# Two expert layers: blocks of 32 tokens for blocks of 64, spread context steps, first rows by a one-hot product, weights fetched in the order of first use

## The chip, the cores and the metric

The kernel runs on one NeuronCore of a Trainium2 chip. The metric is the time of one launch in microseconds (us), as the device counts it; lower is better. TensorE (PE in the profile) multiplies matrices, VectorE (DVE) and ScalarE (ACT) do elementwise work, GpSimd (POOL) issues the gathers and scatters, and SyncE (SP) issues all other transfers. Everything is fp32.

## The reference, cut to what matters

Two transformer blocks run one after the other over 512 tokens of width 1024. The first ends in an expert layer; the second has a mixer over a short context sequence and the tokens, and then an expert layer of its own. Both expert layers have 32 experts in 4 groups. A token picks one group and two experts in it, so there are 1024 assignments, and each is a gated product through three matrices of 2 MiB:

```python
grp = argmax(logits_c)                       # 1 of 4 groups
top_val, top_idx = top_k(logits_f[grp], 2)   # 2 of its 8 experts
gate = softmax(top_val) * w_grp
y[tok] += gate * ((silu(x @ w_gate[e]) * (x @ w_up[e])) @ w_down[e])
# w_gate, w_up: (32, 1024, 512); w_down: (32, 512, 1024)
```

For the inputs of the reference the experts get from 12 to 49 rows in the first layer, and from 1 to 100 in the second, where five get more than 64.

## The kernel before, in words

The program is written engine by engine: each engine has its own list of instructions, and semaphores tie the lists together. A weight matrix of an expert is one 2 MiB transfer on SyncE's queue into one of several buffers. In the first layer (`m = 0`) these are the six buffers of `ring`, so two experts' weights fit; in the second layer (`m = 1`) four areas of `arena` join them, which makes ten. `STREAM[m]` (line 214) is the order of the 96 transfers of a layer and `SPOT` (line 224) says which buffer each takes; `load_e` (line 1293) waits until the buffer's last user is done and issues the transfer. That last user is the gate and up product of the expert's last block for a gate or up matrix, and the down product for a down matrix (`spent`).

**Blocks.** `BLOCKS[m]` is a fixed list of blocks of `CAP` = 64 rows, each belonging to one expert position: 32 blocks in the first layer, 38 in the second, where six positions have two. In the second layer the experts are first ranked by their row counts, so that the large ones take the positions with two blocks (`RANK`, `order`, `homes`); the first three (`FIXED`) keep their places, since their weights are fetched before the counts are known. An expert with more rows than its blocks hold is finished by a loop at the end of the layer, in overflow blocks: every engine goes through `Fori(0, NOV)` with an `If`, and `NOV` is 15. In the profile nothing runs inside that loop.

**One block on TensorE** (`experts` of the tensor list, lines 847 to 946) is: `gate_up` (868, 870), with the weights as the moving operand of 512 columns, gate into partitions 0 to 63 of a PSUM bank and up into 64 to 127; `turn_x` (855), eight transposes of the next block's rows; `down` of the block before (884, 886); `turn_h` (895), four transposes of the hidden rows. ScalarE does the silu (1837), copies the turned hidden rows (1842) and, in the first layer, the result (1831); VectorE multiplies by up (2542), scales the turned rows (2385, 2389) and, in the second layer, takes the result times its share and a gain (2377). GpSimd gathers each block's rows from a copy of the normalized tokens in DRAM (1476) and scatters the results as half rows (1485).

**Beside the first layer** the second block's work on the context sequence runs: `context()` is a generator on each engine, and TensorE, ScalarE and VectorE take two of its 64 steps in every block (`next(beside, None)`).

**Head of a layer.** VectorE and TensorE compute the routing; the first two blocks' token numbers come from a small product (`first_slots`, 1006), GpSimd gathers these rows, and `gate_up(0)` follows. SyncE, after storing the normalized tokens (1363), waits for the second gather before it goes on to the context's transfers (1366 to 1369) or the stream of weights.

**End of a layer.** After the overflow loop GpSimd scatters the last two blocks, SyncE loads the results back by token (`load_y`, 1306), and VectorE adds them to the residual: lines 2604 and 2605 after the first layer, 2816 and 2817 after the second.

## Time and profile before

| | us |
|---|---|
| median of 3 runs | 1801.9 (1799.53 to 1804.74) |
| the profiled execution | 1797.79 |
| its span, first to last instruction | 1796.0 |
| TensorE busy | 1673.9 (93% of the span) |
| VectorE busy | 657.9 (37%) |
| ScalarE busy | 444.3 (25%) |
| granted clock of TensorE, mean | 0.968 of full speed |
| moved by DMA | 519.45 MB, 289 GB/s over the span |

All times in the profile count from the first instruction. The first expert layer lies at about 340 to 876, the mixer of the second block from there to about 1250, the second expert layer to 1772. Matmuls are pipelined, so the time from the start of one to the start of the next says more than the duration shown. An fp32 product is two records, and a line in the profile is that of the kernel before.

### The profile page before, as it was taken

Reading aid. Unit: us, or ns where it says so; the run is one execution under the profiler, and the core shown is the slowest. Engines: PE = TensorE matmul, PEld = TensorE weight load, DVE = VectorE, ACT = ScalarE, POOL = GpSimd, SP = SyncE. Lnnn points to the kernel's source line nnn. Section 1 sums busy time; section 2 is a strip of 40 time slices with the busy share of each in tenths; the row PEclk is TensorE's granted clock in tenths of the full one; section 3 lists DMA queues with packets and bytes.
Section 4 is the critical chain, followed back from the end, with each engine's and each line's share of the span. In section 5 each row is a group of like instructions: output and inputs, shape, how many; then the busy total and the mean of one; then the engine's idle time right before and its main releaser. Section 6 shows DMA issues by size and latency. Waiting matters only on the chain.

```text
span 1796.0 us, 21821 instructions
## 1 busy us (share of the span) xinstructions
PE 1673.9 (93%) x8694; PEld 857.8 (48%) x8694; DVE 657.9 (37%) x1266; ACT 444.3 (25%) x803; POOL 170.5 (9%) x172
## 2 busy tenths in 40 slices
PE   7999999799999999999699997999799999999993
PEld 3455454445445555455345557965433333333331
DVE  3279341432222212122469937542522222221213
ACT  2233771133221112111348412232000000000001
POOL 0000000011111111110000013100111111111100
PEclk9999999799999999999899998999799999999987
DMA  9265531499999999999470191055899999999995
GB/s 366 101 241 182 189 141 47 152 399 402 393 408 405 406 405 399 403 413 410 175 270 1 13 137 48 1 227 216 318 394 396 404 410 399 409 419 411 423 421 214
DMA packets 95324, 519.45 MB, mean 289 GB/s; under 512 B 22509, under 2 KB 28237, under 8 KB 70648
## 3 DMA queue, kind: packets, MB, share of 16 engines
q1 hardware_dynamic: 84024, 500.66, 72.0%
q0 software_dynamic: 11200, 17.39, 2.9%
q8 instruction: 71, 1.16, 0.3%
q14 instruction: 29, 0.24, 0.0%
HBM read 508.19 MB, written 29.15 MB: 299 GB/s over the span
## 4 chain that ended last, share of the span: by engine, by line
PE 69%; DMA 14%; issue 8%; DVE 5%; ACT 2%; SPq 2%; DVEq 0%; POOLq 0%
PE bank L868 22%; PE bank L884 11%; PE bank L461 8%; PE bank L469 7%; DMA ring<-in_w_up 6%; PE bank L825 3%; PE bank L855 3%; DMA ring<-in_w_down 2%; DMA arena<-in_w_down 2%; PE bank L895 2%; PE bank L527 2%; PE bank L692 2%; PE bank L454 1%; DVE arena L2643 1%; DMA ring<-diag 1%
## 5 line engine op out<-in xcount | busy, mean ns | idle before, releaser
L870 PE MATMUL bank<-ring,arena 128*64 128x512 f32 x912 | 413.2, 607 | 0.0
L868 PE MATMUL bank<-ring,arena 128*64 128x512 f32 x896 | 402.9, 603 | 7.9 <-DMA ring<-in_w_up 4.6
L2542 DVE TENSOR_TENSOR arena<-arena,bank 64x512 f32<-64x512 f32 x70 | 48.3, 690 | 557.5 <-ACT arena L1837 557.5
L461 PE MATMUL bank<-arena,ring 128*128 128x512 f32 x560 | 244.6, 593 | 0.0
L868 PEld LDWEIGHTS bank<-ring,arena 128*64 128x64 f32 x896 | 119.7, 139 | 243.3 <-issue 236.7
L884 PE MATMUL bank<-ring,arena 128*64 128x512 f32 x424 | 193.2, 598 | 2.0 <-DMA ring<-in_w_down 2.0
L886 PE MATMUL bank<-ring,arena 128*64 128x512 f32 x424 | 193.2, 598 | 0.0
L1476 POOL DMA_INDIRECT arena<-xnd,smalli x70 | 67.8, 969 | 1051.1 <-PE bank L855 535.3
L1837 ACT ACTIVATE arena<-bank 64x512 f32<-64x512 f32 x70 | 41.3, 590 | 509.9 <-PE bank L870 509.9
L461 PEld LDWEIGHTS bank<-arena,ring 128*128 128x128 f32 x560 | 105.2, 190 | 127.0 <-issue 127.0
L870 PEld LDWEIGHTS bank<-ring,arena 128*64 128x64 f32 x912 | 122.5, 139 | 0.0
L469 PE MATMUL bank<-arena 128*128 128x128 f32 x880 | 112.4, 280 | 0.0
L469 PEld LDWEIGHTS bank<-arena 128*128 128x128 f32 x880 | 103.0, 192 | 18.4 <-issue 16.9
L868 PE MATMUL bank<-arena 128*64 128x512 f32 x224 | 102.2, 610 | 6.1 <-DMA ring<-in_w_up 6.1
L884 PEld LDWEIGHTS bank<-ring,arena 128*64 128x64 f32 x424 | 53.8, 136 | 96.8 <-issue 91.1
L1485 POOL DMA_INDIRECT yd<-arena,smalli x70 | 70.1, 1001 | 301.4 <-DVE arena L2377 159.3
L870 PE MATMUL bank<-arena 128*64 128x512 f32 x208 | 92.0, 595 | 0.0
L855 PEld LDWEIGHTS bank<-mats,arena 64*128 64x128 f32 x560 | 67.0, 199 | 47.2 <-issue 43.2
L855 PE MATMUL bank<-mats,arena 64*128 64x64 f32 x560 | 76.6, 278 | 11.5 <-DMA arena<-xnd,smalli 11.5
L2643 DVE SCALAR_TENSOR_TENSOR arena<-arena,par 128x512 f32<-128x512 f32 x96 | 72.2, 752 | 3.4
L1842 ACT ACTIVATE arena<-bank 128x256 f32<-128x256 f32 x70 | 26.9, 385 | 179.0 <-PE bank L895 178.6
L895 PEld LDWEIGHTS bank<-mats,arena 64*128 64x128 f32 x280 | 38.7, 209 | 55.3 <-issue 55.2
(452 smaller groups left out, 2104.8 us busy)
## 6 DMA issues: line engine op xcount, KB each, us to landing
ring<-in_w_up SPq DMA_DIRECT2D x53, 2048.0 KB, 20.6
ring<-in_w_gate SPq DMA_DIRECT2D x52, 2048.0 KB, 17.6
ring<-in_w_down SPq DMA_DIRECT2D x50, 2048.0 KB, 20.0
arena<-in_w_down SPq DMA_DIRECT2D x14, 2048.0 KB, 36.4
ring<-in_w_mod SPq DMA_DIRECT2D x12, 2048.0 KB, 15.5
arena<-in_w_gate SPq DMA_DIRECT2D x12, 2048.0 KB, 34.6
arena<-in_w_up SPq DMA_DIRECT2D x11, 2048.0 KB, 27.4
ring<-in_w_in SPq DMA_DIRECT2D x10, 2048.0 KB, 17.4
```

The source lines that it names most:

```text
L461: mm = pe.matmul(b[:, 0:n], w[:, k, col:col + P], ap[:, k, :], start=(k == 0), stop=(k == KD - 1))
L469: mm = pe.matmul(hd(b, h), lhs(h) if callable(lhs) else hd(lhs, h), rhs(h) if callable(rhs) else hd(rhs, h), start=True, stop=True)
L825: mm = pe.matmul(banks[t][:, :], yT(k)[:, P * t:P * t + P], w[:, k, :], start=(k == 4), stop=(last and k == ks[-1]), skip_group_check=True)
L855: mm = pe.transpose(XT[:, CAP * c:CAP * c + CAP], xg[u][:, c::KD], M["ident"][0:CAP, 0:CAP])
L868: pe.matmul(GU[0:CAP, :], x, wg_[:, c, :], start=(c == 0), stop=(c == KD - 1), skip_group_check=True)
L870: mm = pe.matmul(GU[CAP:2 * CAP, :], x, wu_[:, c, :], start=(c == 0), stop=(c == KD - 1), skip_group_check=True)
L884: pe.matmul(Y[0:CAP, :], x, wd_[:, c, 0:512], start=(c == 0), stop=(c == 3), skip_group_check=True)
L886: mm = pe.matmul(Y[CAP:2 * CAP, :], x, wd_[:, c, 512:1024], start=(c == 0), stop=(c == 3), skip_group_check=True)
L895: mm = pe.transpose(HT[:, CAP * c:CAP * c + CAP], hb[u][:, c::4], M["ident"][0:CAP, 0:CAP])
L1476: pool.indirect_dma_start(out=xg[u], out_offset=None, in_=xnd[m], in_offset=bass.IndirectOffsetOnAxis(ap=slots_any[:, n:n + 1], axis=0), b ...
L1485: pool.indirect_dma_start(out=halves, out_offset=bass.IndirectOffsetOnAxis(ap=homes_any[:, n:n + 1], axis=0), in_=ys[u], in_offset=None, b ...
L2643: ins = STT(o8, pad[:, j // 3:j // 3 + 8, j % 3:j % 3 + 64], pcol("cw2", 9 * n + j), o8, ALU.mult, ALU.add)
```

## The change

- Blocks hold 32 rows. `gate_up` and `down` use four column groups of 32 and moving operands of 256 columns, where there were two of 64 and 512. `SIZES` gives each position 1 to 4 blocks: 52 in the first layer, 56 in the second. Both layers now rank the experts.
- Rows are gathered, turned, scaled and scattered for four blocks at a time (`QUAD`, 128 rows), whole rows of 4 KB; `take_y` is four copies of 32 rows by 256 columns. The share of an assignment is applied when the results are added.
- The first 64 rows of the experts 0 and 1 come from a product of the normalized tokens with a one-hot matrix (`first_x`), not from a gather.
- The 64 context steps are placed at chosen points of the blocks (`BESIDE`), so that the work per expert position comes out even.
- `STREAM` is sorted by TensorE's first use, in both layers. A down matrix is fetched in two halves per partition.
- `NOV` is 31; overflow blocks have 128 rows. The waits on SyncE for the first gathers are gone; the load into the tokens' buffer waits for the second `first_x` product.

```diff
-CAP = 64
-NOV = 2 * T // CAP - 1
+CAP = 32
+QUAD = P // CAP
+SIZES = [[2, 2, 2, 1, 1] + [2, 2, 1] * 8 + [2, 1, 1],
+         [2, 2, 2, 1, 1, 1] + [3, 1, 4, 1, 3, 1, 3, 1, 3, 1] + [2, 2, 1] * 4 + [2, 2, 1, 1]]
+NOV = 31
+CONTEXT_STEPS = 64
+PLACES = [[(0, "after"), (0, "down"), (0, "turn"), (0, "half")],
+          [(1, "half"), (0, "down"), (1, "down"), (0, "turn"), (0, "after"), (1, "after")]]
...
+        def first_use(m, j, p):
+            return 2 * FIRSTB[m][p] + (3 if j == 2 else 0), j
+        STREAM = [sorted([(j, p) for j in range(3) for p in range(NE)], key=lambda u: first_use(m, *u)) for m in range(2)]
-        SPOT = [0, 1, 2, 3, 4, 6, 7, 5, 8, 9]
+        SPOT = [0, 1, 2, 3, 4, 6, 7, 5, 9, 8]
...
+                def first_x(e):
+                    b = CV.deal(pe, f"first{m}{e}")
+                    if e == 0:
+                        pe.wait_ge(S("placed"), 3 * m + 1)
+                        pe.wait_ge(S(f"xn{m}"), TT)
                     for c in range(KD):
+                        for t in range(TT):
+                            mm = pe.matmul(b[:, 2 * CAP * c:2 * CAP * c + 2 * CAP], xn_tok[:, t, c::KD], in_soon[:, TT * e + t, :],
+                                           start=(t == 0), stop=(t == TT - 1), skip_group_check=True)
+                    mm.then_inc(CV.full, 1)
+                def turn_x(q, half):
+                    pe.wait_ge(S("xs_ready"), 2 * (g0 + q) + half)
+                    if half == 0:
+                        pe.wait_ge(S("gathered"), 16 * (GBASE[m] + q))
+                    for c in range(4):
+                        mm = pe.transpose(hd(XT, c), xg[:, 4 * half + c::KD], M["ident"])
...
                     for c in range(KD):
-                        x = xTs[u][:, CAP * c:CAP * c + CAP]
-                        pe.matmul(GU[0:CAP, :], x, wg_[:, c, :], start=(c == 0), stop=(c == KD - 1),
+                        if c == KD // 2 and beside_now(n, "half"):
+                            next(beside, None)
+                        x = xTs[q % 2][:, P * c + CAP * b:P * c + CAP * b + CAP]
+                        for i, (w, col) in enumerate(((wg_, 0), (wg_, 256), (wu_, 0), (wu_, 256))):
+                            mm = pe.matmul(GU[CAP * i:CAP * i + CAP, 0:256], x, w[:, c, col:col + 256],
+                                           start=(c == 0), stop=(c == KD - 1), skip_group_check=True)
...
+                        for i in range(4):
+                            mm = pe.matmul(Y[CAP * i:CAP * i + CAP, 0:256], x, wd_[:, c, 256 * i:256 * i + 256],
+                                           start=(c == 0), stop=(c == 3), skip_group_check=True)
...
+                first_x(0)
+                homes()
+                pe.wait_ge(V.free, len(V.names))
                 for n in range(last + 1):
                     gate_up(n)
                     if n == 0:
+                        first_x(1)
+                    if n == 1:
+                        spots()
+                    if beside_now(n, "after"):
                         next(beside, None)
+                    half = turns_at(m, n)
+                    if half is not None:
+                        turn_x(n // QUAD + 1, half)
                     if n:
                         down(n - 1)
+                    if beside_now(n, "down"):
+                        next(beside, None)
                     turn_h(n)
+                    if n == 0:
+                        slots()
+                    if beside_now(n, "turn"):
                         next(beside, None)
                 down(last)
...
-                sp.wait_ge(S("gathered1"), 16 * (BASE[m] // 2 + 1))
                 if m == 0:
                     sp.dma_start(hTc, a["ctxT"].rearrange("(c p) t -> p c t", p=P)).then_inc(S("ctx_in"), 16)
                     sp.dma_start(wkc, cols(a["w_in_2"], 2)).then_inc(S("ctx_w"), 16)
                     sp.wait_ge(S("xn_out"), 16 * TT)
+                    sp.wait_ge(CV.full, CV.at("first01"))
                     sp.dma_start(wvc, cols(a["w_in_2"], 3)).then_inc(S("ctx_w"), 16)
                 if m:
-                    sp.wait_ge(S("xn_out"), 16 * TT * 2)
+                    sp.wait_ge(S("x2_out"), 16 * (1 + TT))
                     load_e(1, 8)
...
+                    if p >= FIXED and j == 0:
+                        if p == FIXED:
+                            sp.wait_ge(S("ordered"), m + 1)
+                        expert[p] = sp.value_load(ordt[0:1, r:r + 1], min_val=0, max_val=NE - 1)
                     if m and i == 3 * FIXED:
-                        sp.wait_ge(S("x2_out"), 16 * (1 + TT))
+                        sp.wait_ge(S("xn_out"), 16 * TT * 2)
+                        sp.wait_ge(CV.full, CV.at("first11"))
                     load_e(m, i, expert.get(p))
...
+                    for i in range(4):
+                        ins = A(ys[q % 2][CAP * b:CAP * b + CAP, 256 * i:256 * i + 256], Y[CAP * i:CAP * i + CAP, 0:256],
+                                ACT.Copy)
...
-                chain(TTo(o, o, yg[t][0], ALU.add))
-                TTo(o, o, yg[t][1], ALU.add).then_inc(S("x4_ready"), 1)
+                chain(STT(o, yg[t][0], w12[:, t:t + 1], o, ALU.mult, ALU.add))
+                STT(o, yg[t][1], w12[:, TT + t:TT + t + 1], o, ALU.mult, ALU.add).then_inc(S("x4_ready"), 1)
```

## Rows read from the trace of the kernel before

**Rows 1.** Busy time by stretch: microseconds (count) per engine, granted clock, DMA share, GB/s
```profile
353.00:866.00 513.00, 513.00 (x2796) 260.35 (x2792) 119.18 (x217) 116.86 (x203) 59.00 (x60) 1.00 0.98 395
1500.00:1740.00 240.00, 226.72 (x1082) 89.29 (x1080) 50.85 (x72) 17.54 (x36) 34.33 (x35) 0.97 1.01 416
```

**Rows 2.** Waits of SyncE's queue: waits for whom, total, times, longest
```profile
SPq L1301 <- PE bank L870: 593.7, 59, 24.6
```

**Rows 3.** Groups by line, 1500 to 1760: count, busy, mean, idle before
```profile
L868 PE MATMUL bank<-ring,arena 128*64 128x512 f32 x204 | 92.9, 609 | 5.3 <-DMA ring<-in_w_up 4.6 <-DMA arena<-in_w_up 0.7
```

**Rows 4.** Timeline of TensorE, one block of the first layer: start, duration, line
```profile
837.33 0.64 PE L868 MATMUL bank<-ring,arena 128*64 128x512 f32 x1
...
844.35 2.05 PE L469 MATMUL bank<-arena 128*128 128x128 f32 x16
...
846.33 1.09 PE L855 MATMUL bank<-mats,arena 64*128 64x64 f32 x8
...
847.35 0.64 PE L884 MATMUL bank<-ring,arena 128*64 128x512 f32 x1
...
850.94 0.69 PE L895 MATMUL bank<-mats,arena 64*128 64x64 f32 x4
...
851.56 2.05 PE L469 MATMUL bank<-arena 128*128 128x128 f32 x16
...
853.54 0.64 PE L868 MATMUL bank<-ring,arena 128*64 128x512 f32 x1
```

**Rows 5.** Timeline of TensorE, modulation by four column groups
```profile
178.46 1.93 PE L639 MATMUL bank<-ring,smallf 128*2 128x128 f32 x64
```

**Rows 6.** DMA queues, 330 to 870: packets, MB, share
```profile
q0 software_dynamic: 5040, 8.64, 4.7%
```

**Rows 7.** Timeline at the first layer's head
```profile
342.47 0.69 DVE L2446 TENSOR_TENSOR arena<-par,arena 128x512 f32<-128x512 f32 x1
...
352.31 1.11 PE L868 MATMUL bank<-ring,arena 128*64 128x512 f32 x1 [0.88 <-DVE arena L2385]
...
361.83 0.34 SPq L1301 DMA_DIRECT2D ring<-in_w_up  x1
```

**Rows 8.** Timeline at the second layer's head
```profile
1260.55 1.75 PE L993 MATMUL bank<-arena,mats 128*128 128x128 f32 x8
...
1263.74 0.69 DVE L2446 TENSOR_TENSOR arena<-par,arena 128x512 f32<-128x512 f32 x1
...
1275.72 0.36 SPq L1301 DMA_DIRECT2D arena<-in_w_gate  x1
...
1276.06 1.11 PE L868 MATMUL bank<-ring,arena 128*64 128x512 f32 x1 [1.69 <-DVE arena L2389]
```

**Rows 9.** Groups of the page: busy, mean ns, idle before
```profile
L1842 ACT ACTIVATE arena<-bank 128x256 f32<-128x256 f32 x70 | 26.9, 385 | 179.0 <-PE bank L895 178.6
```

**Rows 10.** Timeline after the first layer
```profile
861.30 0.69 DVE L2542 TENSOR_TENSOR arena<-arena,bank 64x512 f32<-64x512 f32 x1 [13.14 <-ACT arena L1837]
...
870.22 0.69 DVE L2175 TENSOR_TENSOR arena<-arena,smallf 128x512 f32<-128x512 f32 x1 [8.23 <-issue]
...
873.80 0.97 POOL L1485 DMA_INDIRECT yd<-arena,smalli  x1 [5.21 <-ACT arena L1831]
...
879.71 1.28 ACT L1872 ACT_TABLE_LOAD   x1 [6.68 <-issue]
...
883.08 1.28 DVE L2604 SCALAR_TENSOR_TENSOR arena<-ring,smallf,arena 128x1024 f32<-128x1024 f32 x1 [8.31 <-DMA ring<-yd]
...
885.72 1.06 ACT L1876 ACTIVATE arena<-arena 128x1024 f32<-128x1024 f32 x1 [4.73 <-DVE arena L2605]
```

**Rows 11.** Timeline of VectorE at the end
```profile
1766.94 0.75 DVE L2377 SCALAR_TENSOR_TENSOR arena<-bank,smallf,arena 128x512 f32<-128x512 f32 x1 [4.04 <-PE bank L886]
...
1777.13 1.23 DVE L2816 TENSOR_TENSOR arena<-arena 128x1024 f32<-128x1024 f32 x1 [9.44 <-DMA arena<-yd]
...
1787.67 4.99 DVE L2821 SCALAR_TENSOR_TENSOR arena<-arena,smallf 128x1024 f32<-128x1024 f32 x5
```

More of the change, by code:

```diff
@@ L434, in settle, with stores, beside_now, turns_at @@
                 eng.sem_inc(S(f"passed_{eng.engine.name}"), 1)
+        def stores(m, q):
+            return sum(len(range(q % 2, NQ[i], 2)) for i in range(m)) + q // 2
+        def beside_now(n, at):
+            return (n, at) in BESIDE
+        def turns_at(m, n):
+            b = n % QUAD
+            half = b - 2 if n < QUAD else b - 1
+            return half if half in (0, 1) and n // QUAD + 1 < NQ[m] else None
         block = ctx.enter_context(nc.Block())
@@ L1025, in moe @@
                               start=True, stop=True).then_inc(V.full, 1)
-                experts(m)
+                experts(m, homes)
             moe(0)
@@ L1444, in _ @@
             load_e(1, 3)
+            for r in range(QUAD):
+                part, at = slice(CAP * r, CAP * r + CAP), 5 * D + 256 * r
+                sp.dma_start(m5[part], modd[0:1, at:at + 256].partition_broadcast(CAP)).then_inc(S("rows"), 16)
+                sp.dma_start(b5[part], a["bmod"][:, at:at + 256].partition_broadcast(CAP)).then_inc(S("rows"), 16)
             sp.wait_ge(S("outB_ready"), TT)
@@ L1449, in _ @@
             sp.wait_ge(S("y_taken"), BASE[1] + NB[1])
-            for q in range(2):
-                sp.wait_ge(S(f"stored{q}"), 16 * ((BASE[1] + NB[1]) // 2))
+            for u in range(2):
+                sp.wait_ge(S(f"stored{u}"), 16 * stores(2, u))
             sp.wait_ge(S("yd_done"), 2)
@@ L1488, in scatter @@
                         .then_inc(S(f"stored{u}"), 16)
-                for n in range(NB[m] + 2):
-                    if n == 2:
-                        pool.wait_ge(CV.free, CV.at(f"slots{m}"))
-                    if n < NB[m]:
-                        gather(n)
-                    if n == 4:
-                        pool.wait_ge(CV.free, CV.at(f"spots{m}"))
-                    if n >= 4:
-                        scatter(n - 4)
+                pool.wait_ge(CV.free, CV.at(f"slots{m}"))
+                gather(1)
@@ L1500, in experts @@
+                gather(2)
+                pool.wait_ge(CV.free, CV.at(f"spots{m}"))
+                for q in range(3, NQ[m]):
+                    scatter(q - 3)
+                    gather(q)
+                scatter(NQ[m] - 3)
                 baton = S(f"beyond{m}")
@@ new lines, in take_y, with first_x @@
+                    for i in range(4):
+                        ins = TTo(ys[q % 2][CAP * b:CAP * b + CAP, 256 * i:256 * i + 256], Y[CAP * i:CAP * i + CAP, 0:256],
+                                  m5[CAP * i:CAP * i + CAP, :], ALU.mult)
+                    ins.then_inc(S("y_taken"), 1)
+                def first_x(e):
+                    b = take(f"first{m}{e}", CV)
+                    o, o3 = chunks(xTs[0], P)[:, :, 2 * CAP * e:2 * CAP * e + 2 * CAP], [P, KD, 2 * CAP]
+                    ins = TTo(o, chunks(b[:, :], 2 * CAP), bc(gain, 2, o3), ALU.mult)
+                    ins.then_inc(CV.free, 1)
+                    if shift is not None:
+                        own(f"first{m}{e}", CV)
+                        ins = TTo(o, o, bc(shift, 2, o3), ALU.add)
+                        ins.then_inc(S("xs_ready"), 1)
+                    else:
+                        own(f"first{m}{e}", CV)
+                        dve.sem_inc(S("xs_ready"), 1)
@@ new lines, in experts @@
+                dve.wait_ge(S("ranked"), m + 1)
+                dve.sem_inc(V.free, 1)
+                dve.wait_ge(S("gains"), 1 + 2 * m)
+                first_x(0)
+                b = take(f"homes{m}")
+                CP(bc_row, b[:, 0:2 * NE])
+                chain(CP(ordt, b[0:1, 2 * NE:3 * NE]))
+                dve.sem_inc(S("ordered"), 1)
+                dve.sem_inc(V.free, 1)
+                home, cap, many = bc_row[:, 0:NE], bc_row[:, NE:2 * NE], key[:, 0:NE]
+                chain(TTo(many, cnt, cap, ALU.subtract))
@@ L2478, in experts @@
+                o3 = [P, NE, OVER]
+                chain(TTo(over, bc(many, 2, o3), bc(pcol("slot0", 0, OVER), 1, o3), ALU.is_gt))
                 chain(dve.tensor_reduce(nov, over, AX, ALU.add))
```

523 lines of the change are left out of this document (233 added, 290 removed).

## The prediction

> **What bounds the kernel now.** I read the table by stretch first. In the first expert layer TensorE is busy in all of 353 to 866, 513.00 of 513.00 us, at full granted clock; the DMA engines are booked nearly full too, but move 395 GB/s [rows 1]. To see which of the two sets the pace I took the waits of SyncE's queue: it waits 59 times, 593.7 us in all, for TensorE to free a weight buffer [rows 2]. So weights are fetched no faster than TensorE uses them, and the 395 is a demand, not a limit. In 1500 to 1740 of the second layer it is the other way round: TensorE is busy 226.72 of 240 us, the transfers run at 416 GB/s [rows 1], and the gate and up products wait for weights (4.6 us for ring, 0.7 for arena) [rows 3]. I take 416 for what the transfers can do.
>
> TensorE's timeline of one first-layer block shows where its time goes: gate and up 844.35 − 837.33 = 7.02, a context step 1.98, turning rows 1.02, down 3.59, turning hidden rows 0.62, a second step 1.98, from 837.33 to 853.54, or 16.21 us [rows 4]. 32 such blocks are 519 us. The reference's counts matter: in the second layer five experts have more than 64 rows, and all have a block list that holds them before and after, so no overflow block runs in either kernel.
>
> **The change part by part.**
>
> *Blocks of 32 rows.* An fp32 product is two records; I count records. gate_up is now 16 pairs of records of 512 columns, a pair side by side in two column groups, in 7.02 us, and down 8 pairs in 3.59; the difference is 3.43/8 = 0.429 a pair, which leaves 0.15 for the ends [rows 4]. So 512 columns take 0.429 however many column groups run, and 128 a quarter of it, 0.107. What four groups do the modulation shows: 64 records of 128 columns, 16 quads, in 1.93 us, 0.121 a quad [rows 5], 0.013 over 0.107. After the change gate_up is 16 quads of 256 columns and down 8; a quad is 0.215 + 0.013 = 0.228, gate_up 16 × 0.228 + 0.15 = 3.8, down 8 × 0.228 + 0.15 = 2.0 us. Turning hidden rows is half as many transposes, 0.35 for 0.62; rows are turned once for four blocks, eight records of 0.128 (below), 0.26 a block for 1.02. A block costs 6.4 us where it cost 12.25 [rows 4].
>
> First layer: 52 × 6.4 = 333, the 64 steps as before 64 × 1.98 = 127, first_x(1) with 32 products or 64 records at 0.128 (a context step's 2.05/16 [rows 4]) 8.2, slots and spots 4: 472 us of TensorE, for 519. Bounds for a quad: 0.214 (no excess) and 0.27 (the excess grows with the columns, and TensorE's instruction list doubles, whose fetching no row shows). Placing the steps evenly costs nothing by itself: a position of one block gets up to four steps and one of two blocks mostly one, 14 to 15 us each, so that weights can flow steadily.
>
> *The weights.* With 472 us of work TensorE no longer lies above the transfers. 96 matrices of 2.097 MB, 6 of them there at the start, leave 90 × 2.097 = 188.7 MB; the gathers and scatters move 8.6 MB beside them [rows 6], less the two first gathers and the same bytes in whole rows: 8.2. Together 196.9 MB at 416 GB/s, 473 us. The two sums are equal, so the one that starts later decides, and it is the stream.
>
> *The head of the first layer.* The routing ends at 342.47 + 0.69 = 343.2 and gate_up starts at 352.31, after gather, turning and scaling [rows 7]. Ranking is new here and puts three small VectorE operations ahead of the one-hot matrix, 0.9 us: 344. first_x(0) is 64 records; TensorE has just waited, and after such a wait eight took 1.75 us, 0.219 each [rows 8], where 0.128 is the price in full flow. I take 20 at the first and 44 at the second, 10 us (8 and 14 are the ends): 354, scaling 0.7, gate_up(0) at 355, 3 later than now. An expert's first buffers come free with its last block: 3.8, first_x(1) 8.2, turn_h 0.35, down 2.0, a step 2.0, gate_up 3.8 make 375, where the first refill goes out at 361.83 [rows 7]. With 2 us until its packets flow the stream runs from 377, and +473 its last matrix lands at 850. By the new order two down matrices stand behind the last up matrix, 10 us, so that one lands at 840; then come gate_up 3.8, four steps 7.9, two downs 4.0, turn_h 0.35 and 0.9 of handing over: TensorE ends at 857. Four copies on ScalarE instead of one are 4 × 0.385 = 1.5 [rows 9], so ScalarE ends at 858.5 and the scatter is issued at 859.5; it stood at 873.80 [rows 10]: −14.3. Within the stretch copies, multiplications and scalings lie beside TensorE's 6.4 us a block; without that cover the copies alone would cost 1.5 us a block, 78 us.
>
> *The overflow loop* runs with no block in it 31 times instead of 15. It shows as VectorE's 8.23 us and ScalarE's 6.68 us of idle without a releaser [rows 10]: 0.55 and 0.45 a turn, so 17.0 and 13.8 us. VectorE's last multiplication lies about 848 (TensorE has 9 us of other work behind it), so it is out at 865, does what now takes from 870.22 to 874.77 (883.08 less its wait of 8.31) and is ready at 869.4; the loaded results come 9.3 us after the scatter (883.08 − 873.80) [rows 10], at 868.8. So 2604 runs at 869.4 for 883.08. ScalarE comes out at 858.5 + 13.8 + 1.3 for the table load = 873.6, where its line 1876 starts at 885.72 [rows 10]: **−12.1 us**, 2.2 of the 14.3 being the loop's. Bounds: −9 if a turn is dearer in the new code, −14 if it is hidden.
>
> *The second layer.* first_x(0) replaces the first gather: from the one-hot matrix at 1263.74 + 0.69 to gate_up at 1276.06 are 11.6 us [rows 8], about what 64 records and the scaling take by the prices above; no change. The load into the tokens' buffer waits for first_x(1), so the stream's next matrix goes at 1276 + 3.8 + 8.2 = 1288 where it went at 1275.72 [rows 8]; one load passes it, early. Left are 87 matrices and 8.1 MB of rows, 190.5 MB, at 416 GB/s 458 us: 1747. TensorE's work, 56 × 6.4 = 358, fits beside it, and its granted clock would have to fall to 0.78 on the mean before it didn't. Then 2.0 for down, 1.5 for copies and 1 of handing over: the last copy ends at 1751.6, where the last take_y ends at 1766.94 + 0.75 [rows 11], −16.1. Here VectorE takes the results, so its loop begins after them: out at 1768.6, when the results have been back by token since 1751.6 + 9.4 = 1761 (the 9.44 of its wait now). It starts line 2816 at 1768.6 for 1777.13, and its eight additions, all ready, take 8 × 1.28 = 10.3 where 10.54 pass now to line 2821 [rows 11]: **−8.8 us**. The loop gives half of the 16.1 back. What follows is as it was.
>
> *Single edits at little or nothing.* Down in two halves per partition: shorter rows, from nothing to 1% of the stream (5 us a layer), as no row shows its price; I take none. Ranking in the first layer: in the 0.9 above, and homes on TensorE behind first_x. The share is applied where results are added, by an operation of the shape of 2604. The waits that SyncE loses stood ahead of the context's transfers; behind its new waits for first_x queue the weights, counted above. Gathers of four blocks at once are POOL's, a quad ahead of their use, beside TensorE's 25 us a quad.
>
> The sum is −12.1 − 8.8 = −20.9 us. The profiled execution took 1797.79 with a span of 1796.0, so 1775 and 1777; the median of the runs stands 4 above the profiled one, so **1781 us**. For the transfers I allow 395 to 428 GB/s (3% over 416) in the first layer (+25 to −13 us) and, where 416 is the layer's own row, 404 to 428 in the second (+14 to −13). TensorE's and the transfers' equal sums in the first layer add some waiting on either side; a faster stream would be half eaten by the loops. With a quad of 0.214 to 0.25 that makes 1766 to 1797 for this case.
>
> **The rivals.**
> *A, slower: the quad.* If four column groups share less than the modulation shows, a quad of 256 costs 0.28, a third over 0.214, and a block 24 × 0.28 + 0.3 + 0.61 = 7.63 us. TensorE then has 397 + 139 = 536 us in the first layer and ends at 355 + 536 = 891; ScalarE comes through its copies, loop and table at 891 + 16.6 = 907.6, +21.9, less 8.8 for the second layer, which still hangs on weights: +13, **1815 us**. It decides from a quad of 0.27, where the two layers cancel (355 + 523 + 16.6, +8.9). Against it stand 0.121 for 0.107 [rows 5]; for it, that those records have two rows of output and 128 columns, and that twice as many instructions must be fetched. 14%.
> The Trainium skill (TensorE: Matmul & The Clock Gate, Part 3: Packing small matmuls) has three column tiles at 2.38 times and four row tiles at 3.07 times one; by it a quad is, as an estimate, 0.214 × 4/3.07 = 0.28 us, rival A's time. The trace's quad speaks for 3.5 times.
> *B, no change: the ring.* If six buffers can't carry 416 GB/s, because TensorE holds about three and a freed one needs issue and flight, the first layer stays at 395: 498 us from 377 are 875, TensorE ends 7 later at 882, ScalarE is through at 898.6, +12.9, less 8.8: +4, **1806 us**. For it: no stretch of the first layer shows more than 395 [rows 1]; against: SyncE waited for TensorE there [rows 2]. 13%.
> *C, faster: cheap turns.* If a loop's turn costs half in the new code, 2 us come back in the first layer and 7 in the second, where the results by token then come last: 1772. 7%.
> That the change doesn't do what it says would be overflow blocks; the counts exclude them.
>
> **How the numbers follow.** Forecast 66%, A 14, B 13, C 7. 0.3% is 5.4 us, what a measurement can tell; faster means under 1796.5, slower over 1807.3. The forecast (but 1 in 100) and C are faster: 0.73; B mostly the same: 0.13; A slower: 0.14. The range must leave out 2 in 10: 1760 (a stream of 428 in both layers) to 1808, with B in and A out.
>
> **What would show it.** Right: quads start every 0.23 us and a block takes 6.4; the first layer moves 410 to 420 GB/s with TensorE waiting for weights now and then; gate_up(0) at 355 and the first refill at 375; last scatter at 860; VectorE idle 17 us without a releaser after each layer, ScalarE 14; the second layer's additions begin at 1756.5 (1768.6 less the 12.1 won before). Wrong: quads of 0.27 and a SyncE that still waits for TensorE all the time (A), 395 GB/s with both waiting (B), a turn of the loop far from 0.55, a first refill past 380, or a second layer whose stream falls under 404.

## The result, and the profile after

The changed kernel takes 1838.61 us (median of 4, 1831.76 to 1840.74) for 1801.76: a ratio of 1.0197, with a 95% interval of 1.0166 to 1.0228. It is slower by 37 us where a gain of 21 was forecast. The profiled execution has a span of 1838.1 us for 1796.0, and its milestones show where the 42 us arise. The forecast's own times stand in the middle; from the second layer on they count on its new clock, 12.1 us earlier. The rank product is TensorE's first product in a layer's ranking of the assignments; the head of a layer is counted from it.

| us from the first instruction | before | forecast | after |
|---|---|---|---|
| first layer: rank product | 339.7 | – | 344.0 |
| first layer: gate_up(0) | 352.3 | 355 | 365.8 |
| first refill of a weight buffer | 361.8 | 375 | 394.9 |
| last scatter issued | 873.8 | 859.5 | 896.9 |
| ScalarE goes on behind the layer | 885.7 | 873.6 | 910.2 |
| second layer: rank product | 1260.0 | – | 1288.3 |
| second layer: gate_up(0) | 1276.1 | 1263.9 | 1310.4 |
| load into the tokens' buffer | 1275.7 | 1275.9 | 1331.4 |
| last result taken | 1767.7 | 1739.5 | 1804.2 |
| additions begin | 1777.1 | 1756.5 | 1819.7 |

First the table by stretch, with the columns of [rows 1]:

```profile
340.00:400.00 60.00, 54.48 (x376) 47.15 (x380) 21.07 (x84) 6.29 (x17) 1.19 (x1) 0.63 0.44 153
356.00:386.00 30.00, 29.44 (x169) 26.49 (x168) 8.20 (x25) 0.38 (x1) 0.00 (x0) 0.61 0.01 2
400.00:880.00 480.00, 432.41 (x5714) 282.17 (x5710) 106.02 (x207) 168.17 (x394) 23.65 (x23) 0.97 0.99 407
1302.00:1331.00 29.00, 28.22 (x162) 25.00 (x161) 8.84 (x26) 0.38 (x1) 0.00 (x0) 0.62 0.00 1
1360.00:1780.00 420.00, 337.83 (x4948) 196.53 (x4940) 138.42 (x298) 32.70 (x100) 24.19 (x24) 0.89 1.01 423
```

And the kernel before in the stretches that answer to the first and the fourth of these:

```profile
340.00:400.00 60.00, 52.60 (x300) 27.76 (x301) 23.29 (x73) 16.02 (x27) 7.83 (x8) 0.86 0.85 325
1264.00:1302.00 38.00, 29.67 (x219) 15.76 (x218) 19.52 (x55) 1.56 (x3) 5.26 (x5) 0.81 0.85 299
```

Inside the layers the transfers are what was hoped for in the second, 423 GB/s, and near it in the first, 407. But for some 30 us at each head they stand still, 2 and 1 GB/s, while TensorE is busy nearly all of the time, at a granted clock of 0.61 and 0.62. The kernel before moved 325 GB/s in 340 to 400, where 153 are left, and 299 over its second head. TensorE's timeline of the first head, which answers to [rows 7], and SyncE's first refill say what it is busy with:

```profile
344.04 0.77 PE L1028 MATMUL bank<-arena,mats 128*128 128x128 f32 x2 [5.25 <-DVE arena L2491]
...
348.58 15.52 PE L882 MATMUL bank<-arena 128*128 128x64 f32 x64 [0.23 <-issue]
...
365.83 4.89 PE L911 MATMUL bank<-ring,arena 128*32 128x256 f32 x64 [0.56 <-DVEq L2531]
370.65 15.49 PE L882 MATMUL bank<-arena 128*128 128x64 f32 x64
...
386.49 3.64 PE L943 MATMUL bank<-arena 128*128 128x45 f32 x16
390.06 4.72 PE L911 MATMUL bank<-ring,arena 128*32 128x256 f32 x64
...
398.87 3.66 PE L911 MATMUL bank<-ring,arena 128*32 128x256 f32 x64
...
403.11 1.93 PE L927 MATMUL bank<-ring,arena 128*32 128x256 f32 x32
```

```profile
386.23 0.37 SPq L1407 DMA_DIRECT2D arena<-in_w_in  x1
394.85 0.34 SPq L1327 DMA_DIRECT2D ring<-in_w_gate  x1
...
405.10 0.38 SPq L1327 DMA_DIRECT2D ring<-in_w_down  x1
413.02 0.35 SPq L1327 DMA_DIRECT2D ring<-in_w_gate  x1
```

L882 is first_x, 64 records, 15.5 us each time; L911 is gate_up, L943 the product for the slots, L927 down. No weight buffer is free until the second block of expert 0 is through gate_up, at 394.7. In steady flow the quads cost what they were forecast at or a little less: gate_up's 16 take 3.66 us at 398.87, 0.229 each with the ends in it, where 3.8 us were forecast, and down's 8 take 1.93 for 2.0. The second head, in the place of [rows 8]:

```profile
1292.97 15.47 PE L882 MATMUL bank<-arena 128*128 128x64 f32 x64 [0.39 <-DVE arena L2512]
...
1310.39 5.35 PE L911 MATMUL bank<-ring,arena 128*32 128x256 f32 x64 [0.78 <-DVEq L2531]
1315.67 15.48 PE L882 MATMUL bank<-arena 128*128 128x64 f32 x64
```

```profile
1289.18 0.89 SPq L1327 DMA_DIRECT2D arena<-in_w_down  x1
1331.39 0.35 SPq L1327 DMA_DIRECT2D arena<-in_w_gate  x1
1340.11 0.34 SPq L1327 DMA_DIRECT2D ring<-in_w_up  x1
```

Behind the first layer, where [rows 10] stand for the kernel before (VectorE, POOL, ScalarE, then TensorE), and at the end, in the place of [rows 11]:

```profile
902.36 0.69 DVE L2216 TENSOR_TENSOR arena<-arena,smallf 128x512 f32<-128x512 f32 x1 [16.98 <-issue]
```

```profile
896.91 0.96 POOL L1520 DMA_INDIRECT yd<-arena,smalli  x1 [43.97 <-ACT arena L1865]
```

```profile
908.87 1.28 ACT L1913 ACT_TABLE_LOAD   x1 [12.73 <-issue]
```

```profile
915.50 8.37 PE L1067 MATMUL bank<-arena 128*128 128x128 f32 x48 [20.96 <-issue]
```

```profile
1802.48 1.73 DVE L2420 TENSOR_TENSOR arena<-bank,arena 32x256 f32<-32x256 f32 x4 [2.90 <-PE bank L927]
1819.67 1.28 DVE L2867 SCALAR_TENSOR_TENSOR arena<-arena,smallf 128x1024 f32<-128x1024 f32 x1 [15.47 <-issue]
```

The 31 turns of the overflow loop show as 16.98 us on VectorE and, between the last copy's end at 896.1 and 908.87, 12.7 on ScalarE. TensorE has a loop as well, of 20.96 us, and it comes out last: work goes on at 915.50, 5 us behind ScalarE. Before the change it went on 2.4 us behind ScalarE, and waited for that:

```profile
888.12 7.95 PE L1040 MATMUL bank<-arena 128*128 128x128 f32 x48 [15.73 <-ACT arena L1879]
```

### The profile page after: what moved, and what is told of

Same layout as the page of the kernel before. It is cut to its first block, busy times and chain, and to the rows that moved or that the text cites. A ratio compares the mean times of both kernels' runs of the same rounds, so it can differ in the third digit from the quotient of the medians.

```text
span 1838.1 us, 36358 instructions
## 1 busy us (share of the span) xinstructions
PE 1597.6 (87%) x15456; PEld 999.9 (54%) x15456; DVE 706.0 (38%) x1471; ACT 504.5 (27%) x1055; POOL 85.8 (5%) x84
## 4 chain that ended last, share of the span: by engine, by line
PE 55%; DMA 31%; DVE 6%; issue 3%; ACT 2%; SPq 2%; DVEq 0%; ACTq 0%; POOLq 0%
DMA ring<-in_w_up 18%; PE bank L911 12%; PE bank L485 8%; PE bank L493 7%; DMA arena<-in_w_up 6%; PE bank L927 4%; PE bank L882 3%; PE bank L849 3%; PE bank L1283 3%; DMA ring<-in_w_down 2%; DMA arena<-in_w_down 2%; PE bank L716 2%; PE bank L551 1%; PE bank L478 1%; DMA arena<-xnd,smalli 1%
## 5 line engine op out<-in xcount | busy, mean ns | idle before, releaser
L911 PE MATMUL bank<-ring,arena 128*32 128x256 f32 x5664 | 420.1, 416 | 92.7 <-DMA ring<-in_w_up 70.8
L911 PEld LDWEIGHTS bank<-ring,arena 128*32 128x32 f32 x5664 | 218.9, 119 | 225.8 <-issue 136.1
L911 PE MATMUL bank<-arena 128*32 128x256 f32 x1248 | 134.8, 435 | 28.7 <-DMA arena<-in_w_up 14.5
L927 PE MATMUL bank<-ring,arena 128*32 128x256 f32 x2592 | 156.0, 381 | 3.7 <-DMA ring<-in_w_down 3.7
L927 PEld LDWEIGHTS bank<-ring,arena 128*32 128x32 f32 x2592 | 80.8, 110 | 56.5 <-DMA ring<-in_w_down 5.1
L493 PEld LDWEIGHTS bank<-arena 128*128 128x128 f32 x880 | 103.0, 192 | 15.3 <-issue 14.2
L2420 DVE TENSOR_TENSOR arena<-bank,arena 32x256 f32<-32x256 f32 x224 | 94.2, 420 | 39.2 <-PE bank L927 36.0
L1865 ACT ACTIVATE arena<-bank 32x256 f32<-32x256 f32 x208 | 78.0, 375 | 100.1 <-PE bank L927 98.1
L911 PEld LDWEIGHTS bank<-arena 128*32 128x32 f32 x1248 | 67.0, 125 | 58.6 <-issue 41.1
L882 PE MATMUL bank<-arena 128*128 128x64 f32 x256 | 62.0, 438 | 0.6 <-DVE arena L2512 0.4
L882 PEld LDWEIGHTS bank<-arena 128*128 128x128 f32 x256 | 61.3, 335 | 1.6 <-issue 1.6
L935 PEld LDWEIGHTS bank<-mats,arena 64*128 64x128 f32 x216 | 33.6, 203 | 42.8 <-issue 38.2
L849 PE MATMUL bank<-ring,arena 128*128 128x512 f32 x128 | 55.7, 593 | 0.0
L1283 PE MATMUL bank<-ring,arena 128*128 128x512 f32 x128 | 55.6, 592 | 0.0
```

What stands on the lines that cost most here:

```text
L493: mm = pe.matmul(hd(b, h), lhs(h) if callable(lhs) else hd(lhs, h), rhs(h) if callable(rhs) else hd(rhs, h), start=True, stop=True)
L849: mm = pe.matmul(banks[t][:, :], yT(k)[:, P * t:P * t + P], w[:, k, :], start=(k == 4), stop=(last and k == ks[-1]), skip_group_check=True)
L882: mm = pe.matmul(b[:, 2 * CAP * c:2 * CAP * c + 2 * CAP], xn_tok[:, t, c::KD], in_soon[:, TT * e + t, :], start=(t == 0), stop=(t == TT - ...
L911: mm = pe.matmul(GU[CAP * i:CAP * i + CAP, 0:256], x, w[:, c, col:col + 256], start=(c == 0), stop=(c == KD - 1), skip_group_check=True)
L927: mm = pe.matmul(Y[CAP * i:CAP * i + CAP, 0:256], x, wd_[:, c, 256 * i:256 * i + 256], start=(c == 0), stop=(c == 3), skip_group_check=True)
L1283: mm = pe.matmul(banks[t][:, :], y, w[:, k, :], start=(k == 0), stop=(k == KD - 1), skip_group_check=True)
```

## The experiments

My theory (H) was that the heads did it: the one-hot products stand ahead of the first free buffer, and as the stream is the bound afterwards, each us there is a us of the end. Its rivals: the overflow loops (L), the new order of the weights (O), and a stream or blocks slower than forecast (S).

**The one-hot products undone.** Rows of the first four blocks come by a gather again, for the numbers that a short product (soon_slots, 1.02 us) gives:

```diff
-                first_x(0)
+                soon_slots()
                 homes()
                 pe.wait_ge(V.free, len(V.names))
+                for half in range(2):
+                    turn_x(0, half)
                 for n in range(last + 1):
                     gate_up(n)
-                    if n == 0:
-                        first_x(1)
...
-                    sp.wait_ge(CV.full, CV.at("first01"))
...
+                pool.wait_ge(CV.free, CV.at(f"soon{m}"))
+                gather(0)
```

> The one-hot products undone: the first four blocks' rows come by a gather again, after a product of 16 records for their token numbers; blocks, order of the weights, steps and loops stay as changed. Theory H (the head of each layer: two one-hot products of 15.5 us stand ahead of the first free weight buffer, and the stream, which is the bound afterwards, starts later by as much): the first gate and up product at about 357 for 365.8, the first refill at about 369 for 394.9, in the second layer the load into the tokens' buffer some 40 us earlier; about 25 us less in the first layer and 30 in the second, 1775 to 1795. Theory S (the stream or the blocks are slower inside the layers, the heads are hidden): under 10 us less, 1828 or more.

1821.89 us, 1.0110 of the time before (1.0076 to 1.0143): 17 less than the changed kernel, a third of what H expected. The first refill goes at 380.9 and the last scatter at 883.8, both 13 to 14 earlier, and the second layer's last scatter 19 earlier; so H has the right place. It has not the right size, since the new head is slow itself (below). S is not ruled out: from the first refill to the last scatter 502.9 us pass here, 502.1 in the changed kernel, where the forecast had 484.5; what that is comes further down.

```profile
358.62 1.09 PE L890 MATMUL bank<-mats,arena 128*128 128x128 f32 x4 [7.31 <-DMA arena<-xnd,smalli]
...
362.51 5.49 PE L907 MATMUL bank<-ring,arena 128*32 128x256 f32 x64 [0.79 <-DVE arena L2434]
...
371.98 2.67 PE L939 MATMUL bank<-arena 128*128 128x45 f32 x16 [2.58 <-DVE arena L2548]
374.58 6.27 PE L907 MATMUL bank<-ring,arena 128*32 128x256 f32 x64
```

The gather is waited for 7.31 us, the halves are turned and scaled one after the other, and the product for the slots waits 2.58 us for VectorE ahead of the second block. In the second layer TensorE waits 13.82 us for the gathered rows:

```profile
1295.52 1.09 PE L890 MATMUL bank<-mats,arena 128*128 128x128 f32 x4 [13.82 <-DMA arena<-xnd,smalli]
```

**The same products with neighbouring columns as weights.**

```diff
-  mm = pe.matmul(b[:, 2 * CAP * c:2 * CAP * c + 2 * CAP], xn_tok[:, t, c::KD], in_soon[:, TT * e + t, :],
+  mm = pe.matmul(b[:, 2 * CAP * c:2 * CAP * c + 2 * CAP], xn_tok[:, t, P * c:P * c + P], in_soon[:, TT * e + t, :],
```

> The one-hot products take their weights from 128 neighbouring columns of the tokens instead of every eighth, so the first 64 rows of two experts have their features in another order. Theory W (reading weights at a stride sets 0.242 us a record, at either clock): first_x(1) near 8 us for 15.5 and first_x(0) near 10, the clock stays up for what follows, 25 to 30 us less in all. Theory C (64 moving columns leave the clock at its lower level, and that makes the price): both stay at 14 us or more, under 8 us less in all.

1818.23 us in one run, 20 less: between the two. The two products of the first layer tell why, on TensorE's timeline and in its stretches (columns as in [rows 1]):

```profile
346.73 13.89 PE L882 MATMUL bank<-arena 128*128 128x64 f32 x64 [0.23 <-issue]
...
362.36 5.09 PE L911 MATMUL bank<-ring,arena 128*32 128x256 f32 x64 [0.56 <-DVEq L2531]
367.38 7.36 PE L882 MATMUL bank<-arena 128*128 128x64 f32 x64
```

```profile
350.00:354.00 4.00, 4.00 (x20) 4.00 (x20) 0.00 (x0) 0.00 (x0) 0.00 (x0) 0.50 0.99 368
368.00:372.00 4.00, 4.00 (x38) 4.00 (x38) 3.32 (x6) 0.00 (x0) 0.00 (x0) 1.00 0.00 0
```

first_x(1) takes 7.36 us, 0.115 a record, at full clock: about what the forecast had taken (8.2), and theory W's. But first_x(0) still takes 13.89, 0.217 a record, at a granted clock of 0.50 in all of it although TensorE is busy without a break; the clock rises only in gate_up behind it. So W's price for the stride holds, and for neighbouring columns the clock sets the price. C falls as it was put, since first_x(1) has the same 64 moving columns at full clock; why the clock stays low all through first_x(0) no run shows. The changed kernel adds one thing, seen in two microseconds of its first_x(1) (columns: PE, PEld, granted clock, DMA share, GB/s):

```profile
371.65:372.65 1.00, 1.00 (x6) 1.00 (x6) 1.00 0.00 0
375.65:376.65 1.00, 1.00 (x6) 1.00 (x6) 0.50 0.00 0
```

At a stride the rate is the same at either level, 0.242 a record, and 5 us into the product the clock falls to its lower level under a TensorE that never paused. What comes behind pays as well: the slots cost 3.64 us for 1.98 and gate_up(1) 4.72 for 3.66.

**The loop passed by on VectorE and ScalarE.**

```diff
+                with dve.If(n_over > 0):
                     with nc.vector.Fori(0, NOV) as i:
                         with dve.If(n_over > i):
```

> VectorE and ScalarE pass the 31 turns of the overflow loop by with one test when no block is left over; all else as changed. If the loop costs what its wait behind the results by token leaves: after the first layer about 1 us (the results come 9.3 us after the scatter at 896.9, at 906.2, where the additions start at 906.8), after the second 5.3 (the results at 1814.4, additions at 1819.7): 1832. Theory L (the loops' 17 us lie on the path in full and are what the change lost): 17 us less in each layer, 1805.

1837.74 us, 1.0188 (1.0153 to 1.0223): no difference that can be told. At the end the mechanism is as expected, the additions begin at 1821.93, 9.3 us behind the last scatter, where they began 14.7 behind it, 5.4 us less, and what they wait for is now the results:

```profile
1821.93 1.28 DVE L2869 SCALAR_TENSOR_TENSOR arena<-arena,smallf 128x1024 f32<-128x1024 f32 x1 [10.08 <-DMA arena<-yd]
```

But this run's first layer ended 6 us later, and behind it TensorE's own loop of 21.0 us stayed. Theory L falls. The 6 us are scatter: the code is the same up to there. From the rank product to the last scatter 552.9 us pass in the changed kernel, 558.1 here and 556.8 in all_skip_only (below), so a difference of 5 us in a layer's length between two traces says nothing.

**The old order of the weights.**

```diff
-        STREAM = [sorted([(j, p) for j in range(3) for p in range(NE)], key=lambda u: first_use(m, *u)) for m in range(2)]
+        STREAM = [[], [(0, 0), (1, 0), (0, 1), (1, 1), (2, 0), (0, 2), (1, 2), (2, 1), (2, 2)]]
+        for m in range(2):
+            for p in range(3 * m, NE):
+                STREAM[m] += [(0, p), (1, p)]
+                if p > 3 * m:
+                    STREAM[m].append((2, p - 1))
+            STREAM[m].append((2, NE - 1))
```

> The weights in the order of the kernel before, all else as changed. Theory H: no cause, within 5 us of 1838. Theory O (the order by first use holds buffers back and starves the ring): 15 us less or more.

1877.85 us, 1.0416 (1.037 to 1.0462): 39 slower than the changed kernel, the opposite of O. The first refill is where it was, 394.3, but the first layer's last scatter is at 928.8. Who waits for what on TensorE in 400 to 880, first with the old order (L933 is its down), then in the changed kernel (L927 is down, L911 gate_up):

```profile
PE bank L933 <- DMA ring<-in_w_down: 56.1, 13, 8.5
```

```profile
PE bank L911 <- DMA ring<-in_w_up: 36.3, 14, 5.4
...
PE bank L927 <- DMA ring<-in_w_down: 2.0, 2, 1.3
```

With gate and up ahead of the down matrix that is needed first, down waits 56.1 us, and while TensorE stands there it frees no buffer: the transfers run at 381 GB/s in 400 to 880, where the changed kernel has 407. By first use down waits 2.0. Of the parts of the change that were undone by themselves, the order is the one that pays; the blocks of 32 and the spread of the context steps were not undone alone.

**The gather without company, and the first buffer freed earlier.** gather_first let the context's transfers and a load of weights go before the rows had come. Three more steps, each on top of the last:

```diff
# gather_wait
+                sp.wait_ge(S("gathered"), 16 * (GBASE[m] + 1))
                 if m == 0:
...
# early_release
                     gate_up(n)
                     if n == 1:
+                        slots()
                         spots()
...
                     turn_h(n)
-                    if n == 0:
-                        slots()
# late_steps
-    _now = max(0, min(_due - _done, len(PLACES[_size - 1])))
+    _now = max(0, min(_due - _done, len(PLACES[_size - 1]))) if _p >= FIXED else 0
```

> gather_first (rows of the first four blocks by a gather, 1822 us) with SyncE's wait of the kernel before put back: it sends the context's transfers and the second layer's load of a down matrix only when the first gather has landed. If those transfers held the gather up (it took 7.3 us in the first layer and the tokens' store and it 13.8 in the second, where 5.2 to 5.7 stand before): 2 us less in the first layer, 10 to 12 in the second, 1808 to 1812. If the gather's own size is the cause: no change, 1822.

1811.1 us, 1.0061 (1.0033 to 1.0088): 11 less, as the contention was expected to cost. The wait for the rows is 4.97 us for 7.31 in the first layer and, in the second, 8.04 for 13.82, less of a gain there than the 10 to 12 expected:

```profile
1291.26 1.09 PE L890 MATMUL bank<-mats,arena 128*128 128x128 f32 x4 [8.04 <-DMA arena<-xnd,smalli]
```

> gather_wait, and the products for the slots go behind the second block's gate and up product instead of ahead of it. Theory H (after the head each us until the first weight buffer is free is a us of the end): 5 us earlier in each layer, 10 us less than gather_wait. If TensorE's own work bounds the first layer instead: 5 less at most.

1815.59 us, 1.0087 (1.0053 to 1.0122): no gain, and H as I had put it falls here. The first refill did go 8 us earlier, at 370.87 for 378.99, but the first layer's last scatter is at 882.5 for 881.8. SyncE's timeline shows what was missed:

```profile
370.87 0.34 SPq L1322 DMA_DIRECT2D ring<-in_w_gate  x1
...
390.01 0.38 SPq L1322 DMA_DIRECT2D ring<-in_w_down  x1
398.49 0.35 SPq L1322 DMA_DIRECT2D ring<-in_w_gate  x1
```

Only two buffers come free earlier. The third is a down matrix at 390.0, the next are expert 1's at 398.5, and in gather_first, with its first refill at 380.9, these went at 391.2 and 399.1. With six buffers the start of the stream is the turn of the first two experts, not of the first buffer. The traces bear it out: from the first refill of expert 1's gate buffer to the last scatter pass 483.9 us in the changed kernel (413.02 to 896.91), 484.7 in gather_first, 484.7 in gather_wait and 484.0 here (482 to 488 in all eleven runs that fetch the same matrices in the same order with the same products), while from the very first refill it is 502.1, 502.9, 502.8 and 511.6.

> early_release, and VectorE and ScalarE pass the overflow loop by when no block is left over: 5 us less after the second layer and 1 to 2 after the first, 6 to 7 less than early_release.

1809.53 us, 1.0043 (1.0024 to 1.0062): 6 less, as expected, though the two intervals still overlap.

> early_skip, and no context step beside the first three expert positions (they are made up for later). If the steps there hold back the first buffers: 3 to 6 us less than early_skip. If TensorE has no room for them later, as much more.

1808.53 us, 1.0036 (1.0018 to 1.0055): no difference.

**What sets the first layer's end.** Half the bytes of its down matrices, or half the products of its gate_up:

```diff
# half_down
+                if j == 2 and m == 0:
+                    dst, src = dst[:, 0:1], src[:, 0:1]
# half_gate
+                    kd = KD if m else KD // 2
-                    for c in range(KD):
+                    for c in range(kd):
```

> The changed kernel, but in the first layer only one half of each down matrix is fetched (31 MB less; the first layer's results are wrong by that, the work of every engine is the same). Theory D (the first layer is bound by its transfers, with TensorE's waits and lower clock behind them): it ends 35 to 50 us earlier, where TensorE's own work of some 475 us behind the first product ends, at about 845. Theory T (TensorE's work and the chain of a block set the first layer's end): under 10 us less.

The last scatter goes at 846.7 for 896.9, 50 us earlier (1788.71 us in one run). Of these 4.7 had come up ahead of the layer (its rank product is at 339.3 for 344.0), so the layer itself is 45.5 us shorter. TensorE is busy nearly throughout, and its waits for weights are down from 38 us (400 to 880) to 2.8 (400 to 840). So the transfers bind, and TensorE's own work ends some 45 us below them.

> The changed kernel, but in the first layer the gate and up products run over one half of the features (a block is 1.8 us shorter on TensorE, some 95 us in the layer; its results are wrong by that, the transfers are the same). The first refill then goes 4 to 5 us earlier, at about 390. Theory P (behind the first refill the transfers alone set the first layer's end): the last scatter follows that alone, at 890 to 893. Theory R (TensorE's time for an expert and the transfers' are so near each other that six buffers let each wait for the other): with TensorE far below, the transfers run at 416 to 420 GB/s without a dip and the last scatter is at 868 to 880.

The last scatter goes at 882.5, 14.4 earlier, from a first refill only 2.7 earlier (1827.67 us in one run): between the two, nearer to R. The last scatter and the stretch, of half_down first and then of half_gate:

```profile
846.66 0.96 POOL L1522 DMA_INDIRECT yd<-arena,smalli  x1 [36.82 <-ACT arena L1867]
```

```profile
400.00:840.00 440.00, 428.25 (x5775) 281.53 (x5767) 107.95 (x210) 170.71 (x399) 23.64 (x23) 0.99 0.91 370
```

```profile
882.50 0.96 POOL L1521 DMA_INDIRECT yd<-arena,smalli  x1 [41.81 <-ACT arena L1866]
```

```profile
400.00:860.00 460.00, 359.11 (x4020) 231.76 (x4016) 101.12 (x200) 164.23 (x384) 23.49 (x23) 0.89 1.00 416
```

With half the bytes of down TensorE is the one that is full, with half the products the transfers are, at 416 GB/s for 407 in the changed kernel. Of its 502 us from the first refill to the last scatter 490 are left. Some 12 us were the two waiting for each other; skip_loops and all_skip_only, with the same first layer as the changed kernel, need 505 to 506 us there, so it may be 15. The 490 us that are left, with the transfers at 416 GB/s, are 6 more than the forecast's 484.5.

**The loop passed by on all engines.** On the changed kernel, on early_skip, and with one more edit of the head:

```diff
# all_skip_only, skip_all: so on TensorE, SyncE and GpSimd too
+                with pe.If(n_over > 0):
                     with nc.tensor.Fori(0, (NOV + 1) // 2) as i:
# skip_banks
-                        mm = pe.transpose(hd(XT, c), xg[:, 4 * half + c::KD], M["ident"])
+                        mm = pe.transpose(hd(HT if q == 0 and half else XT, c), xg[:, 4 * half + c::KD], M["ident"])
```

> The changed kernel, with the overflow loop passed by on all engines when no block is left over (skip_loops did it on VectorE and ScalarE alone; TensorE's loop of 21.0 us ends last after the first layer, at 915.5). If TensorE's loop is what stands there: TensorE starts 3 to 5 us earlier behind the first layer, and with the 5.3 us of the second 8 to 10 us less than the changed kernel, about 1829. If not: 5 less.

1832.82 us, 1.0162 (1.0128 to 1.0195): 6 less, where 8 to 10 were expected, and with intervals that overlap the time alone shows no gain. The trace does: TensorE goes on at 910.6, 13.8 us behind the last scatter, where it was 18.6, and ScalarE is what it waits for.

> early_skip with the loop passed by on all engines. TensorE is out of its loop at 901.4 in early_skip, where ScalarE's part is there at about 896: 4 to 6 us less than early_skip, 1803 to 1806.

1801.64 us, 1.0007 (0.999 to 1.0024): 8 less than early_skip. TensorE's first product behind the layer, in early_skip and here:

```profile
901.44 8.51 PE L1062 MATMUL bank<-arena 128*128 128x128 f32 x48 [21.06 <-issue]
```

```profile
894.72 5.60 PE L1063 MATMUL bank<-arena 128*128 128x128 f32 x32 [15.84 <-ACT arena L1920]
```

Its wait is now for ScalarE's result and not for its own loop. It goes on 6.7 us earlier, 5.2 of which it is nearer to the last scatter (13.5 us behind it for 18.7).

> skip_all, with the two halves of the first four blocks' turned rows in two banks, so that the second need not wait for the first one's scaling: 1 to 1.5 us less at each head, 2 to 3 less than skip_all, about the time before.

1801.11 us, 1.0005 (0.9991 to 1.0019): with the interval no different from skip_all, nor from the kernel before. A version that beats it by a measurable time was not found.

## Why the prediction was wrong, step by step

The forecast's sign was wrong, and no rival's mechanism alone turned it: quads cost 0.229 and not 0.27 (A), the stream beats 395 (B). Two terms of its sum failed: the head of each layer, which is the one-hot products and what else TensorE does before weight buffers come free (some 30 us in the two layers), and the stream that was to run in full from the first free buffer (some 27). One of the prediction's own signs of being wrong, a first refill past 380, came with 394.9. From the milestones, the 63 us between the forecast's start of the last additions and the measured one come in this order: 4.5 ahead of the first layer, 6.3 to its gate_up(0), 9.1 to the first refill, 17.5 to the last scatter, −0.8 at ScalarE's loop; 9.9 to the second gate_up(0), 9.0 to the load into the tokens' buffer, 9.2 to the last result, −1.5 at VectorE's loop.

*Ahead of the layer, 4.5 us.* The one-hot matrix is ready at 348.5 and not at 344: 4.4 of it has come up before the routing begins (its rank product starts at 344.04, before the change at 339.65), in code that the change doesn't touch. It is scatter and no cost of the change: in the traces of the other kernels that product starts anywhere from 339.3 (half_down, with the same code up to there) to 346.1 (late_steps).

*"I take 20 at the first and 44 at the second, 10 us", 6 us in each layer.* first_x(0) takes 15.5. The row taken for its price [rows 8] had neighbouring columns as weights, for which 0.22 is right at a clock of 0.50 (contig's first_x(0): 0.217); at the stride it is 0.242, and the shift to 0.128 after 20 records never came.

*"first_x(1) 8.2", 7.3 us in each layer, and what follows it.* Its price was a context step's, 0.128 [rows 4], for weights at a stride of eight columns: 0.242. The bounds of first_x that I gave were 8 and 14, and both products lay above them. Behind it the clock is low, and the slots, which I had in the sum of TensorE's work but not on the way to the first refill, stand there with 3.64 us, and the two gate_ups take 2 us more than forecast. A down and a context step, 4.0 us together, which I had counted there, are not on that way. The first refill comes 20 us late, the load into the tokens' buffer 55, of which 36.6 were brought along from the first layer and about 3 are TensorE's loop behind it.

*"the stream runs from 377, and +473", 17.6 us in the first layer.* From first refill to last scatter it takes 502 us and not 484.5. I let the stream start in full at the first free buffer and gave the sentence on "equal sums" no price. (The 2 us until its packets flow came from no row; after the issue at 1331.39, with the queue empty, they take about 1.) early_release shows that the start is the turn of two experts, and half_gate prices the mutual waiting at about 12 us. Here rival B was right in kind: six buffers carry 407 GB/s, not 416; but it took 395, and it kept the forecast's start at 377. In the second layer from the load to the last result 473 us pass for 463.6, at 423 GB/s: there too the start, with refills at 1340 to 1354, is what the sum left out, as far as the trace shows; no run was made on it.

*The loops.* 17.0 us on VectorE and 12.7 on ScalarE for 17.0 and 13.8: right. TensorE's loop has no term in the forecast, and no line of it stands in [rows 10]: before the change TensorE waits there for ScalarE anyway (15.73 us, to 888.12). At twice the turns it comes out last: about 3 us.

*What held.* The block: from start to start gate_up 3.59, down 1.86, turning hidden rows 0.38 and half of the 0.65 of turning rows (1344.12 to 1350.60 in the second layer) make 6.2 us for the forecast's 6.4; transfers as the bound of both layers (by experiment in the first, by the trace's 423 GB/s in the second); the copies under the cover of TensorE; the second layer's loop behind the results, which gave back what it should (15.47 us of idle at the end). The Trainium skill's 3.07 for four row tiles (TensorE: Matmul & The Clock Gate, Part 3: Packing small matmuls), from which 0.28 us a quad had been estimated, is not borne out by the four column groups here: the trace's quad shows 4 × 0.214 / 0.229 = 3.7 times one with the ends in it, and 4.0 times without them ((3.59 − 0.15)/16 = 0.215 a quad), and the measurement decides.

So the change trades a stretch bound by TensorE, 16.2 us an expert, for one bound by transfers, 15.7 (502 us for 32 experts), and pays at each head about 30 us in which nothing is fetched. Against the kernel before, from the milestones: the heads cost 29 and 27 us more, from the rank product to the first refill and to the load into the tokens' buffer. The layers behind them give back 10 and 19 (the second layer runs at 423 GB/s for 398 to 405 in 1300 to 1480 before). The loops and what lies behind the layers cost 5 and 6, and the 4.4 ahead are scatter: 42 us in all.

## What to carry to other kernels

Where a change makes transfers the bound, price first every instruction between the last prefetch and the buffers of the first round coming free: the time in which the queue is empty is not won back. Take the price of a product from a row with the same stride of its weights and the same number of moving columns, and look at the granted clock in the row. And count an empty loop on every engine that has it, with the engine that comes out last.

## What the runs showed of the hardware that I had not expected

Weights read at a stride of eight columns make a record of 128 × 64 cost 0.242 us at a granted clock of 1.00 and of 0.50 alike; neighbouring columns cost 0.115 and 0.217. TensorE's clock can stay at its lower level (1.2 GHz), or fall to it, while the engine is busy without a break: 13.9 us at 0.50 in first_x(0) of the run with neighbouring columns (contig), and a fall 5 us into the changed kernel's first_x(1). A turn of the overflow loop with no block in it costs TensorE 21.0/32 = 0.66 us, VectorE 17.0/31 = 0.55.
